# One stage for projection, residual, second norm and router logits; modulation weights in 48 pieces

## What is computed

```python
mods  = silu(c)     @ ada_w[i] + ada_b[i]      # (1, 6*1024): sh1, sc1, g1, sh2, sc2, g2
cmods = silu(c_ctx) @ ada_w[i] + ada_b[i]      # the same for the context
h  = rms_norm(x, n1) * (1 + sc1) + sh1         # also hc from xc and cmods
...                                            # split of h @ w_in: two convolutions, two attentions
x  = x + g1 * (concat([ya, yb, yc, yd]) @ w_out)
h2 = rms_norm(x, n2) * (1 + sc2) + sh2
aff = softmax(h2 @ router)                     # 16 experts, each takes its best tokens
x  = x + g2 * expert_choice_ffn(h2, ...)
```

## Time and profile before

| | |
|---|---|
| median of 3 runs | 3748.98 us (3744.74 to 3753.54) |
| the profiled execution | 3747.07 us |
| its span | 3745.3 us |
| busy: PE, DVE, ACT, POOL | 3104.5, 1013.5, 744.6, 381.8 us |

### The profile page before, as it was taken

The page is one execution under the profiler, slowest core; times in us unless marked ns, Lnnn a source line. Parts: engine busy times, 40 slices in busy tenths (PEclk is TensorE's granted clock), DMA queues, the critical chain, the costliest instruction groups (busy, mean ns, idle before and its releaser), DMA issues.

```text
span 3745.3 us, 39500 instructions
## 1 busy us (share of the span) xinstructions
PE 3104.5 (83%) x16284; PEld 1725.8 (46%) x16284; DVE 1013.5 (27%) x1794; ACT 744.6 (20%) x1368; POOL 381.8 (10%) x561
## 2 busy tenths in 40 slices
PE   3798976599999839888387777399989998889997
PEld 0454543333333214453221111288764676648875
DVE  0224732311110041452300000322323474222232
ACT  0113631001000010351100000322211263122221
POOL 1022510011121111140011110000000000000000
PEclk7798888599999959889599999699999979989998
DMA  9120023299999870002499999421311100312130
GB/s 392 57 57 1 0 101 133 82 368 391 389 387 388 315 276 23 1 1 101 155 408 414 415 413 412 148 90 68 124 61 68 68 1 1 116 69 90 68 124 28
DMA packets 141421, 636.91 MB, mean 170 GB/s; under 512 B 11824, under 2 KB 19008, under 8 KB 86000
## 3 DMA queue, kind: packets, MB, share of 16 engines
q1 hardware_dynamic: 121104, 575.58, 38.9%
q0 software_dynamic: 20192, 59.58, 5.2%
HBM read 611.95 MB, written 23.17 MB: 170 GB/s over the span
## 4 chain that ended last, share of the span: by engine, by line
PE 32%; DMA 11%; DVE 3%; issue 3%; ACT 1%; SPq 1%; POOL 0%; DVEq 0%; POOLq 0%; ACTq 0%
PE bank L753 22%; DMA slots<-in_w_up_dram 7%; PE bank L1139 5%; DMA arena<-in_w_down_dram 3%; PE bank L1042 2%; SPq L711 1%; PE bank L1240 1%; PE bank L1229 0%; PE bank L1061 0%; PE bank L1232 0%; DMA arena<-moe_rows 0%; PE bank L1231 0%; DMA arena<-in_ffn_norm_dram 0%; PE bank L784 0%; DVE X L2118 0%
## 5 line engine op out<-in xcount | busy, mean ns | idle before, releaser
L1042 PE MATMUL bank<-slots,HT 128*32 128x512 f32 x4096 | 482.0, 604 | 78.7 <-DMA slots<-in_w_up_dram 40.7
L753 PE MATMUL bank<-slots,HT 128*128 128x512 f32 (+2 forms) x960 | 400.0, 577 | 20.4 <-ACT done_mark L1746 20.4
L1042 PEld LDWEIGHTS bank<-slots,HT 128*32 128x32 f32 x4096 | 122.2, 111 | 402.2 <-issue 246.5
L753 PEld LDWEIGHTS bank<-slots,HT 128*128 128x128 f32 x960 | 182.3, 191 | 229.2 <-issue 204.0
L753 PE MATMUL bank<-hT_high,chunk_high 128*128 128x512 f32 x704 | 277.5, 394 | 8.3 <-DVE low_slots L2159 8.3
L753 PE MATMUL bank<-hT_high,low_slots 128*128 128x512 f32 x704 | 277.9, 395 | 0.0
L753 PE MATMUL bank<-hT_low,chunk_high 128*128 128x512 f32 x704 | 277.0, 394 | 0.0
L1061 PE MATMUL bank<-arena,HT 128*32 128x512 f32 x2048 | 243.8, 596 | 25.3 <-DMA arena<-in_w_down_dram 23.9
L784 PE MATMUL bank<-ident,arena 128*128 128x128 f32 x272 | 62.9, 411 | 222.8 <-DVE arena L1808 144.6
L753 PE MATMUL bank<-HT,slots 128*128 128x512 f32 (+1 forms) x480 | 176.7, 531 | 1.7 <-issue 1.7
L2069 DVE SCALAR_TENSOR_TENSOR arena<-bank,arena 128x512 f32<-128x512 f32 x32 | 24.0, 750 | 516.7 <-issue 284.5
(11 more groups left out here) (339 smaller groups left out, 4246.1 us busy)
## 6 DMA issues: line engine op xcount, KB each, us to landing
slots<-in_w_gate_dram SPq DMA_DIRECT2D x128, 1024.0 KB, 8.6
slots<-in_w_up_dram SPq DMA_DIRECT2D x128, 1024.0 KB, 12.4
arena<-in_w_down_dram SPq DMA_DIRECT2D x128, 1024.0 KB, 12.5
slots<-in_ada_w_dram SPq DMA_DIRECT2D x24, 2048.0 KB, 22.2
slots<-in_w_in_dram SPq DMA_DIRECT2D x15, 2048.0 KB, 11.2
slots<-in_ffn_w_gate_dram SPq DMA_DIRECT2D x10, 2048.0 KB, 8.5
slots<-in_ffn_w_up_dram SPq DMA_DIRECT2D x10, 2048.0 KB, 9.0
slots<-in_ffn_w_down_dram SPq DMA_DIRECT2D x10, 2048.0 KB, 7.8
```

Source lines behind the costliest of these rows:

```text
L753: mm = pe.matmul(out_, lhsT, rhs, start=(n == 0), stop=(n == len(pairs) - 1))
L1042: mm = pe.matmul(bank[32 * j:32 * j + 32, 2 + n, :], xT[:, kk0 + kk, lo:lo + 32], w[n][:, kk, 512 * h:512 * h + 512], start=(pair == 0 and ...
```

## The change

The modulation weights of both layers come as 48 pieces of 1 MB (layer, third, 128-row block) into a ring of four outside the slots; all their products go to bank 7. Pieces 0 to 7 (third 0 of layer 0) are read in the ada stage, 8 to 19 behind the transposes of layer 0's first norms (two per tile, which therefore use six banks), 20 to 47 behind the products of conv_in of layer 0 (two behind a first part, one behind a second), which uses seven banks. Layer 1 has no ada stage. SP issues ten pieces ahead of conv_in's first unit, ten behind the first and the second unit each, and the last 18 behind the third. DVE takes and POOL stores each third on its own; conv_in ends for POOL only when all six are stored.

The stage w_out now also does the second norm, its transposes, the store of its rows and the logits. PE projects tile i + 1 ahead of the transposes of tile i and the logits of tile i - 1. The modulation rows for it (three per stream) are loaded in conv_out. `arena_free` becomes the end of w_out. The norm stages behind it are gone; route starts from logits in bank 6.

```diff
+ADA_PIECES = LAYERS * THIRDS * KD
+ADA_FIRST = 10
+ADA_BANK = 7
-        if stage.name == "conv_out":
+        if stage.name == "w_out":
             arena_free = number + 1
...
+            def load_ada(first, last):
+                for n in range(first, last):
+                    if n >= 4:
+                        sp.wait_ge(sem["ada_read"], n - 3)
+                    l, third, k = n // (THIRDS * KD), n // KD % THIRDS, n % KD
+                    sp.dma_start(ada_pieces[:, n % 4, :], a["ada_w"][l][P * k:P * k + P, 2 * D * third:2 * D * third + 2 * D])\
+                        .then_inc(sem[f"ada_piece{n % 4}"], 16)
...
+                if stage.name == "ada":
+                    load_ada(0, ADA_FIRST)
...
+                    if stage.name == "conv_in" and stage.layer == 0:
+                        at_piece = ADA_FIRST + 10 * j
+                        load_ada(at_piece, at_piece + 10 if j < 2 else ADA_PIECES)
...
+            def ada_piece(n):
+                third, k = n // KD, n % KD
+                pe.wait_ge(sem[f"ada_piece{n % 4}"], 16 * (n // 4 + 1))
+                if k == 0 and third:
+                    pe.wait_ge(sem["ada_taken"], third)
+                for j in range(4):
+                    mm = pe.matmul(bank[32 * j:32 * j + 32, ADA_BANK, :], silu_c[:, k, :], ada_pieces[:, n % 4, 512 * j:512 * j + 512],
+                                   start=(k == 0), stop=(k == KD - 1))
+                mm.then_inc(sem["ada_read"], 1)
```

Behind the transposes of tile t in PE's norm, and behind each part in PE's conv_in:

```diff
+                    if st.facts["turns"] == 3:
+                        for n in range(KD + 2 * t, KD + 2 * t + 2):
+                            ada_piece(n)
...
+                        if st.layer == 0:
+                            at_piece = KD + 2 * (ST + CT) + 3 * c + 2 * part
+                            for n in range(at_piece, min(ADA_PIECES, at_piece + 2 - part)):
+                                ada_piece(n)
```

The new w_out stage on PE:

```diff
+                project_tile(0)
+                for i in range(tiles):
+                    if i + 1 < tiles:
+                        project_tile(i + 1)
+                    turn_rows(i)
+                    if i:
+                        logits(i - 1)
+                logits(tiles - 1)
```

On ACT:

```diff
+                for i in range(tiles):
+                    act.wait_ge(sem["residual"], st.at("residual", i + 1))
+                    step(act.activation(junk[:, :], X[:, i, :], ACT.Square, accum_out=small[:, i:i + 1]))
+                    act.activation(small[:, 8 + i:9 + i], small[:, i:i + 1], ACT.Sqrt, bias=eps[:, :],
+                                   scale=1.0 / D).then_inc(sem["out_root"], 1)
+                    if i:
+                        take_turned(i - 1)
+                take_turned(tiles - 1)
```

On DVE, per tile:

```diff
+                    dve.tensor_tensor(h, flat_bank[:, b * BANK:b * BANK + D], out_mods[:, row, :], ALU.mult)\
+                       .then_inc(sem["projected_taken"], 1)
+                    dve.wait_ge(sem["projected_taken"], st.at("projected_taken", i + 1))
+                    dve.tensor_tensor(X[:, i, :], X[:, i, :], h, ALU.add).then_inc(sem["residual"], 1)
+                    if i:
+                        take_turned(i - 1)
+                    dve.wait_ge(sem["out_root"], st.at("out_root", i + 1))
+                    step(dve.reciprocal(small[:, 16 + i:17 + i], small[:, 8 + i:9 + i]))
+                    step(dve.scalar_tensor_tensor(h, X[:, i, :], small[:, 16 + i:17 + i], out_mods[:, row + 1, :], ALU.mult, ALU.mult))
+                    dve.tensor_tensor(h, h, out_mods[:, row + 2, :], ALU.add).then_inc(sem["rows_ready"], 1)
```

DVE takes third 0 (`take_third(0)`) in ada, 1 at the end of the x norm, 2 and 3 ahead of conv_in's chunks, 4 ahead of chunk 7 and 5 at its end. POOL in conv_in of layer 0, and in w_out:

```diff
+                store_third(1)
+                store_third(2)
+                load_ada_rows(1)
+                for n in range(3, LAYERS * THIRDS):
+                    store_third(n)
+                pool.wait_ge(sem["mods_stored"], 64 * LAYERS * THIRDS)
...
+                for i in range(tiles):
+                    pool.wait_ge(sem["rows_ready"], st.at("rows_ready", i + 1))
+                    if i:
+                        pool.wait_ge(sem["rows_stored"], st.at("rows_stored", 16 * i))
+                    pool.dma_start(h_rows[st.layer][i * P:(i + 1) * P, :], h_ring[:, i % ring, :]).then_inc(sem["rows_stored"], 16)
+                pool.wait_ge(sem["rows_stored"], st.at("rows_stored", 16 * tiles))
```

More of the change, by code:

```diff
@@ L246, in block_one_stages @@
             stages.append(Stage("angles", signals=dict(tables_loaded=16 * 5, angles=1, sines=1, lam_sum=1, lam_exp=1)))
[L247 to L251, removed]
+        if l == 0:
+            stages.append(Stage("ada", l))
         for first, last, row in ((0, ST, 0), (ST, ST + CT, 1)):
-            stages.append(norm_stage("norm", l, range(first, last), row=row, scale=1, shift=0, store=False))
+            stages.append(norm_stage("norm", l, range(first, last), row=row, scale=1, shift=0, store=False, turns=4 if l else 3))
         n_chunks = CONV_COLS // P
@@ L257, in block_one_stages @@
         groups = n_chunks * parts
+        banks = BANKS if l else ADA_BANK
         spans = [(0, 512), (512, 1024), (1024, CONV_COLS)]
@@ L280, in block_one_stages @@
         stages.append(Stage("conv_out", l, bank_uses=[2], signals=dict(centered=1, squared=2, normed=2)))
[L281 to L284, removed]
         stages.append(Stage(
[L286 to L289, removed]
-            stages.append(norm_stage("norm", l, range(ST, ST + CT), row=1, scale=4, shift=3, store=True))
-        stages.append(Stage("route", l, bank_uses=[1, 1, 1 if l == 0 else 0, 1],
-                            signals=dict(logit_exp=1, affinity=1, ranked=1), tiles=tiles))
+            "w_out", l, tiles=tiles,
+            signals=dict(rows_loaded=16 * 3 * (tiles // 2 - 1), projected=tiles, projected_taken=tiles, residual=tiles, out_root=tiles,
+                         rows_ready=tiles, turned_full=tiles, turned_taken=2 * tiles, logits=1, rows_stored=16 * tiles),
+            units=[(weight_unit(a["w_out"][l], (512 * j, 512 * j + 512)), ("projected", tiles - 1)) for j in range(2)]))
+        stages.append(Stage("route", l, bank_uses=[0, 1, 1 if l == 0 else 0, 1],
+                            signals=dict(logits_taken=1, logit_exp=1, affinity=1, ranked=1), tiles=tiles))
         both = tiles > ST
@@ L388, in units_two, with norm_stage @@
     return latent + diff
-def norm_stage(name, layer, tiles, row, scale, shift, store):
+def norm_stage(name, layer, tiles, row, scale, shift, store, turns=4):
     tiles = list(tiles)
@@ L401, in norm_stage @@
             signals[f"h_stored{q}"] = 16 * len(tiles[q::2])
-    return Stage(name, layer, bank_uses=uses, signals=signals, tiles=tiles, row=row, scale=scale, shift=shift, store=store)
+    return Stage(name, layer, bank_uses=uses, signals=signals, tiles=tiles, row=row, scale=scale, shift=shift, store=store, turns=turns)
 def two_blocks_kernel(nc, a, out, stages):
@@ L1812, in norm @@
                 take(len(tiles) - 1)
+                if turns == 3 and tiles[0] == 0:
+                    take_third(1)
             def conv_in(st):
+                banks = st.facts["banks"]
                 parts = st.facts["parts"]
@@ L1994, in w_out @@
             def w_out(st):
[L1995 to L2002 removed]
+                tiles, ring = st.facts["tiles"], h_ring.shape[1]
@@ L2549, in store @@
                 pool.wait_ge(sem["stored"], 16)
-            programs = dict(init=init, ada=ada, norm=norm, qkv=qkv, attend=attend, w_out=w_out, experts=experts,
+            programs = dict(init=init, ada=ada, norm=norm, conv_in=conv_in, qkv=qkv, attend=attend, conv_out=conv_out, w_out=w_out,
+                            experts=experts,
                             combine=combine, store=store, norm_rows=norm, angles=angles)
```

208 lines of the change are left out of this document (121 added, 87 removed).

## The result

The changed kernel takes 3637.39 us (median of 4 runs, 3632.7 to 3640.82); the kernel before takes 3748.53 us beside it (4 runs, 3744.74 to 3753.54). The ratio is 0.9702, 95% interval 0.9685 to 0.9719. The profiled execution took 3640.82 us, 3639.0 of them span, at a mean granted clock of 0.919 (before 0.902). The kernel before, run again beside each group of experiments, had medians from 3747.13 to 3749.25, so medians of different groups can be compared to some 2 us.

The account below looks back on a forecast made before the run. Took PE to bound the long products, DMA the head, and engines waiting in turn the norms and router. Terms -28 + 35.6 - 40.2 - 46.8 - 31 = -110.4 from 3747.1 gave 3636.7, 3639 beside the median; range 3612 to 3672.

Parts of the forecast that it names:

- B: conv_in of layer 0: 28 pieces, hand-overs, the end store and a slow qkv restart add 35.6 us (bounds +30 and +45).
- C: Head of layer 1: shorter combine (20.7) and angles (2.6), no ada stage (16.9); -40.2 us (bounds -30 and -46).
- D: Layer 0, first projection product to last logits: small steps go behind the next tile's projection; -46.8 us (bounds -40 and -52).
- E: Layer 1, the same overlap of projection, second norm and logits: 107.7 us becomes 76.7, -31 (bounds -25 and -35).
- A: Head of layer 0, up to the first convolution product: earlier norm less the pieces' cost; -28 us (bounds -23 and -36).
- The store begins at about 50.1: Head of layer 0: POOL's first store waits for `ctx`, landing at 50.1; it began at 85.45, so 35.3 us gained.
- the two prices: Layer 0's first norms: 12 pieces cost +17.6 us at the low clock or +4 at the high; +12.2 taken.
- The near tie with the last store: End of layer 0's joined stage: POOL's last 512 KB store ends between 635 and 641, the logits at 639.8.
- Small work did not keep the clock low: Rival: pieces, transposes and logits all cost their low-clock price, +43.6 us in all, giving 3682; chance 0.09.
- the combine was paced by DMA: Against a rival: fixed latencies of POOL's loads pace layer 0's combine, 20.7 us of gain lost, 3660; chance 0.13.
- conv_in ran at 1.00 and not at 0.50: Against the slower rival: pieces break up long products, conv_in at 0.50 throughout, +127 us, 3766; chance 0.03.
- More than forecast: Rival: norm pieces all hidden (-8) and both tails at the high clock (-9), giving 3622; chance 0.10.

Follow-up runs that it names:

- twice: Changed kernel, with each of the 28 pieces in conv_in adding its four products a second time with zeros as the left side; 3661.7 us (0.9772).
- late_store: Changed kernel, with the last modulation store waited for in qkv instead of conv_in's end, and DVE taking the last third inside chunk 10; 3633.1 us (0.9694).
- combine_load: Changed kernel, with SP reading layer 1's 24 MB of modulation weights again, for nobody, during layer 0's combine; 3668.16 us (0.9794).
- no_overlap: Changed kernel, with the joined stage in plain order, one tile after the other: projection, transposes, logits; 3749.61 us (1.0001).
- warm_tail: Changed kernel, with four products for nobody in PE's idle gap behind the last projection of both joined stages; 3633.92 us (0.9697).
- best: Changed kernel, with a separate semaphore for the context tokens (`ctx`), plus the edits of late_store and tail; 3617.15 us (0.9652).
- tail: Changed kernel with warm_tail's products, and SP holding the second 4 MB of expert 0's first weights until the h rows are stored; 3629.99 us (0.968).

## Why the prediction was right

Forecast 3639, measured 3637.39. Runs show the cause for the price of the pieces and for the end store in B (twice, late_store), for the combine in C (combine_load) and for the overlap in D and E (no_overlap). A and the rest of B are read from the rows of the traces, with nothing taken away alone; the last 16.9 us of C are simply a stage that is no longer there.

**A, -28 against -27.1: right in sum by errors that cancel, which is luck.** DVE began its norm 43.4 us earlier (101.24 to 57.79), where 40.2 was forecast. "The store begins at about 50.1" was too late by 5.2: `ctx` landed 32.4 us after its issue and not 37.8. Why is not shown; DMA was at a share of 1.02 in both stretches, with 407 and 413 GB/s. About 2 us of that were lost again, since the store's way to the norm stage took 6.8 us and not 4.5. The pieces cost 10.9: from DVE's first instruction to the end of the x norm 22.3 us instead of 14.6, and in the context norm from there to conv_in's first product 11.5 instead of 8.3. That is close to the 12.2 that were taken between the two prices, and far from the 4 of the high clock: each norm began at the low pace, and one piece came 2.07 us late. What no step of the prediction had was the context norm's load of two modulation rows: 10.7 us instead of 5.3, so +5.4, at a DMA share of 1.01 (second window above), behind the pieces and the w_in unit that the change lets SP issue then. The prediction counts four pieces and a unit "behind the new start" and looks no further than the first norm. -43.4 + 10.9 + 5.4 = -27.1.

**B, +35.6 against +38.4.** Pieces: 1.86 us from start to start for a pair and 1.00 for one alone, 26.9 in all against 25.2; twice adds another behind each for 0.86. Hand-overs: 1.00 + 1.38 = 2.4 against 2.6, at the two places named. The end store: 5.95 of wait against 1.06, so +4.9, and the slow start of qkv +2.5 (92.9 from its first product to its end, 90.4 before); late_store takes exactly these 7.4 away, where 5.8 + 2 were forecast. The rest, 1.7, had no term: between pieces a chunk's 16 + 16 instructions take 7.06 + 3.65 = 10.7 us from start to start, 107.1 for ten, where PE spent 105.5 on all of them before, with a slow first chunk in it. This part is read from the rows and not tested.

**C, -40.2 against -44.0: mechanism right, two sizes low.** The combine ended 26.3 us after POOL's first load (1259.18 to 1285.5), 26 was forecast. But that load came 10.6 us behind the end of the experts; it was put at 1297, 14.5 behind it, about where it stood before. It waits for the experts' last rows to land in DRAM, and that too was quicker with DMA less busy: POOL waited 5.51 us instead of 8.32, and 8.42 again in combine_load. So the combine lost 23.6 us instead of 20.7. A reload took 3.7 us (1270.33 to 1274.01), forecast 4.2. The angles lost 3.5 against 2.6.

**D and E, -46.8 and -31 against -47.8 and -30.8.** Both by the working given: no wait of PE between projections, 0.9 and 1.7 us for the small steps, a gap of 4.29 ahead of the last transposes and 6.84 for the last logits. In layer 0 the last projection ended 93.1 us after the first product, 93.2 forecast, and the tail behind it took 15.6, 16.4 forecast. The near tie with the last store was real and is what warm_tail ran into. no_overlap shows that the overlap earns all of it. Two small slips stand in the working: the steps of D give 156.6 - 109.6 = 47.0 and not 46.8, and the last logits of layer 1 ended at 1828.6 (1814.77 and 13.81 us), not at the window's edge of 1829.4, so E's own steps give -30.2.

The sentence of the Trainium skill that was weighed (TensorE: Matmul & The Clock Gate, Part 4) says that transposes do not engage the higher clock. It does not hold for transposes between long products: eight took 1.04 us there, in a stage with a clock of 0.96, against 1.97 behind an idle stretch. Transposes alone, in the norm of the earlier trace rows, stood at 0.50, as the page has it.

The prediction's first reading, "mostly on TensorE", leans on a chain that was followed through 51% of the span only. No term is taken from it.

**The rivals.** Small work did not keep the clock low (0.96 in the joined stage), though the head of each first norm and both tails ran at the low pace; the combine was paced by DMA; conv_in ran at 1.00 and not at 0.50. "More than forecast" did not come either: the pieces of the norms were not hidden. best gets below its 3622, but by waits of which only the tails' clock was in this rival.

**Open.** Why the attends, unchanged, take 3 to 6 us more or less from profile to profile; why `ctx` landed sooner; why layer 0's last logits stay at 5.55 us in tail where layer 1's take 3.66; and why the experts of layer 1 gained 2.1 with the weights held back.

## What to carry to other kernels

Cost a fusion by what its overlap covers, in both ways: here the joined stage without the overlap is 34 us dearer than the separate stages, since each pause also brings the next long product back at the lower clock. When a big transfer is moved out of one stage, look at every small load of the stage it moves to, up to the last one, and ask what is issued just ahead of it; the same store of 512 KB at the end of layer 1's joined stage took 8.2 us in warm_tail and 3.0 in tail by that alone. And when a wait is taken away with no effect, read which engine's mark ends the stage now, and take away the two together.

## What the runs showed of the hardware

A store of 512 KB on POOL's queue took 3.0 us to POOL's mark with nothing else moving (tail, 1710.86 to 1713.85, at 175 GB/s, which is the store alone), and 7.1 and 7.8 in the changed kernel behind 4 MB that SP had issued within the 8 us ahead of it; with that load it took 7.0 to 8.9 in the traces of all experiments that have the joined stage. The Trainium skill (DMA: Bandwidth & Descriptors, section Anatomy of one DMA) gives for one such DMA 2.0 us plus its bytes at 436 KB a us, an estimate of 3.2 for 512 KB; the idle case is near it, and the loaded ones lie outside that rule.

The eight instructions of a piece with 32 columns took 1.00 us from start to start alone between long products, 0.93 each in a pair, and 0.86 when zeros on the left were added behind real data, and the granted clock stayed at 1.00, which is the 2.4 GHz level. Four products for nobody, 3.68 us together, behind the last projection and its small steps kept the transposes at 1.09 us where 4.29 us of idle had brought them to 1.97.
